# Down projection of a SwiGLU block by seven block products in place of eight, in three chunks between gate/up tiles

## The reference, cut to what matters

```
gate, up = split(rmsnorm(x, g_ffn) @ w_gate_up, 2)      # 1024 -> 2 x 2816
x = x + (silu(gate) * up) @ w_down                      # 2816 -> 1024
```

## Time and profile before

| | us |
|---|---|
| median of 3 runs (1534.44 to 1538.4) | 1536.0 |
| profiled execution, first to last instruction | 1535.0 |
| gate/up and down of layer 0 | about 373 to 779 |
| gate/up and down of layer 1 | about 1100 to 1519 |
| TensorE busy, share of the span | 96% |
| VectorE, ScalarE, GpSimd busy | 43%, 38%, 34% |

### The profile page before, as it was taken

How to read it: one execution, slowest core, us unless ns; L and a number is a source line. 1 busy time by engine, 2 the same in 40 slices (tenths; PEclk the granted TensorE clock), 3 DMA queues, 4 the chain that set the end, 5 groups by cost and what they waited for, 6 DMA issues and landing times.

```text
span 1535.0 us, 27449 instructions
## 1 busy us (share of the span) xinstructions
PE 1471.1 (96%) x10463; PEld 1394.0 (91%) x10463; DVE 656.7 (43%) x1035; ACT 576.1 (38%) x1054; POOL 525.5 (34%) x251
## 2 busy tenths in 40 slices
PE   5899999899999999999999999988999999999996
PEld 5788888699999999999987888868999999999996
DVE  6678777722333333311237666664233333330002
ACT  5454444433222222222235766774422222222211
POOL 1512112134444444344441111112544444443442
PEclk9999999999999999999999999999999999999998
DMA  6223432112222222222231222211222222222231
GB/s 251 72 63 100 130 125 92 56 56 91 81 82 81 81 81 82 86 77 86 78 94 38 89 88 82 71 57 41 83 83 82 82 82 82 82 79 82 83 89 72
DMA packets 42877, 130.25 MB, mean 85 GB/s; under 512 B 5148, under 2 KB 7196, under 8 KB 42688
## 3 DMA queue, kind: packets, MB, share of 16 engines
q1 hardware_dynamic: 38160, 121.23, 26.0%
q10 hardware_dynamic: 4656, 8.21, 1.4%
HBM read 118.85 MB, written 10.57 MB: 84 GB/s over the span
## 4 chain that ended last, share of the span: by engine, by line
PE 83%; DVE 7%; ACT 4%; issue 2%; DMA 1%; DVEq 1%; ACTq 1%; SPq 0%; POOL 0%; POOLq 0%
PE acc L556 72%; PE out_ps L668 4%; PE score L626 3%; PE turned L640 2%; DVE work_c L1160 2%; DMA w_raw<-in_w_in 1%; ACT w_hi L840 1%; PE out_ps L679 1%; DVE work_a L1164 1%; DVE work_a L1157 1%; DVE qz L1133 1%; DVE least L1191 1%; ACT work_c L921 1%; ACT work_c L919 1%; DVE work_b L1198 1%
## 5 line engine op out<-in xcount | busy, mean ns | idle before, releaser
L473 POOL TENSOR_TENSOR w_lo<-w_raw,w_hi 128x1024 fp32r<-128x1024 f32 (+1 forms) x190 | 462.5, 2434 | 856.4 <-ACT w_hi L840 855.9
L556 PE MATMUL acc<-xg_hi,w_hi 128*128 128x288 f32 x2048 | 463.2, 308 | 0.8 <-POOL w_lo L473 0.8
L840 ACT ACTIVATE w_hi<-w_raw 128x1024 fp32r<-128x1024 f32 (+1 forms) x194 | 202.2, 1042 | 640.5 <-PE acc L556 626.4
L556 PE MATMUL acc<-xg_hi,w_lo 128*128 128x288 f32 x2048 | 438.6, 296 | 0.0
L556 PE MATMUL acc<-xg_lo,w_hi 128*128 128x288 f32 x2048 | 437.9, 295 | 0.0
L556 PEld LDWEIGHTS acc<-xg_hi,w_hi 128*128 128x128 f32 x2048 | 332.3, 189 | 20.8 <-issue 13.4
L556 PEld LDWEIGHTS acc<-xg_hi,w_lo 128*128 128x128 f32 x2048 | 329.6, 189 | 0.0
L556 PEld LDWEIGHTS acc<-xg_lo,w_hi 128*128 128x128 f32 x2048 | 329.1, 188 | 0.0
L556 PE MATMUL acc<-f_hi,w_hi 128*128 128x288 f32 x704 | 151.1, 296 | 0.0
L556 PE MATMUL acc<-f_lo,w_hi 128*128 128x288 f32 x704 | 149.8, 293 | 0.0
L556 PE MATMUL acc<-f_hi,w_lo 128*128 128x288 f32 x704 | 148.9, 293 | 0.0
(11 more groups left out here) (148 smaller groups left out, 1620.1 us busy)
## 6 DMA issues: line engine op xcount, KB each, us to landing
w_raw<-in_w_gu SPq DMA_DIRECT2D x88, 512.0 KB, 3.6
w_raw<-in_w_in SPq DMA_DIRECT2D x40, 512.0 KB, 6.0
w_raw<-in_w_dn SPq DMA_DIRECT2D x32, 512.0 KB, 3.5
w_raw<-in_w_out SPq DMA_DIRECT2D x16, 512.0 KB, 3.6
w_raw<-in_w_dn SPq DMA_DIRECT2D x16, 384.0 KB, 3.1
out_k_o<-kb ACTq DMA_DIRECT2D x12, 288.0 KB, 5.1
out_v_o<-vf_z ACTq DMA_DIRECT2D x12, 288.0 KB, 6.9
kb<-in_ck SPq DMA_DIRECT2D x12, 256.0 KB, 2.6
```

The costliest lines, as they stand in the source:

```text
L473: pool.tensor_tensor(w_lo[par][:, 0:cols], raw(s, par, cols), w_hi[par][:, 0:cols].bitcast(F32), ALU.subtract).then_inc(wlo_made, 1)
L556: mm = pe.matmul(acc[:, tpar, h, 0:c1 - c0], w[par][:, k * P:(k + 1) * P], a[:, c0:c1], start=first and n == 0, stop=last and n == 2)
L840: act.activation(w_hi[par][:, 0:cols], raw(s, par, cols), ACT.Copy).then_inc(whi_made, 1)
```

## The change

The input features of the down projection are cut into three chunks of 6, 8 and 8 tiles, and each chunk is multiplied as soon as its gate/up pairs are done: gate/up 0 to 5, down of chunk 0, gate/up 6 to 13, down of chunk 1, gate/up 14 to 21, down of chunk 2. Inside a chunk, each pair of output tiles (4 pairs) is a 2x2 block product: two output tiles by two halves of the chunk's input tiles (3 or 4 tiles each), times two halves of the tokens. Such a product is made of seven block products in place of eight (Strassen, in Winograd's form): the factors are sums and differences of blocks, and the results are added into x piece by piece.

- Weights: three DMAs for each pair bring four blocks of 128 x 384 or 128 x 512 into `d_raw`. GpSimd makes four sums (`d_sum`). For each of the 7 products ScalarE makes `d_hi` and **VectorE** makes `d_lo`, in a ring of three.
- Activations: for an even j VectorE makes one difference of 288 columns, for an odd j a double difference and one more, and ScalarE and VectorE split two blocks (even) or five blocks (odd, 1440 columns) into `f_hi`, `f_lo`. The `high` and `low` of the gate/up slabs stay as they were; the two slabs after a chunk are split around the start of its down products.
- TensorE: a product is 3 x 3 or 3 x 4 matmuls of 288 columns into one bank. Several products accumulate in one bank, and each is added into x by a VectorE operation of 288 columns (`d_add`) before the next goes on top. Loops over gate/up are unrolled on ScalarE and VectorE, and the products are unrolled on all engines.

The diff, cut to its core:

```diff
-DOWN_CUTS = (8, 8, 6)
+CHUNKS = (6, 8, 8)
+CHUNK0 = (0, 6, 14)
...
+PRODUCTS = 7
...
+RING = 3
+QCOLS = 4 * P
...
+    f_hi = sb("f_hi", [P, PRODUCTS, QT, HALF], F32R)
...
+    f_new = sb("f_new", [P, 8, HALF])
+    d_raw = sb("d_raw", [P, 4, QCOLS])
+    d_sum = sb("d_sum", [P, 2, QCOLS])
+    d_hi = sb("d_hi", [P, RING, QCOLS], F32R)
...
+    ADD_TO = ((0, 0), (1, 1), (0, 1), (0, 0), (1, 1), (0, 1), (1, 0))
...
+    def d_bank(pair, r):
+        if r % 2 == 0:
+            return score[:, pair % 2, 0:HALF]
+        return turned[:, 0:HALF] if r == 3 else out_ps[:, 0:HALF]
...
# SyncE, blocks(chunk, m): waits dlo_made and sums_made of the pair before, then
+                sp.dma_start(d_raw[:, 0:2, 0:cols], 
+                             w_dn[layer, 2 * m:2 * m + 2, :, first].rearrange("a p c -> p a c")).then_inc(d_in[0], 16)
...
# GpSimd: first() and second() likewise
+                def third():
+                    pool.wait_ge(dlo_made, pair * PRODUCTS + 2)
+                    pool.wait_ge(sums_made, pair * 4 + 2)
+                    pool.tensor_tensor(one, a11, a21, ALU.subtract).then_inc(sums_made, 1)
...
+                def fourth():
+                    pool.wait_ge(dlo_made, pair * PRODUCTS + 3)
...
+                for t in range(2 * CHUNK0[chunk] + 2, ahead):
+                    if t == ahead - 1:
+                        first()
+                        second()
+                    low(gu_slab(layer) + t, t % 2)
+                third()
+                for t in nxt[0:1]:
+                    low(gu_slab(layer) + t, t % 2)
+                fourth()
+                for t in nxt[1:2]:
+                    low(gu_slab(layer) + t, t % 2)
+                for m in range(1, OUT_PAIRS):
+                    for made in sums(chunk, m):
+                        made()
+                    if chunk == len(CHUNKS) - 1:
+                        for n in range(2 * m - 2, 2 * m):
+                            add_square(2 * layer + 2, n)
...
# TensorE, down(chunk, m), product r
+                    pe.wait_ge(dlo_made, n + 1)
...
+                    elif r == 2:
+                        pe.wait_ge(x_added, pair * PRODUCTS + 1)
+                    elif r == 4:
+                        pe.wait_ge(x_added, pair * PRODUCTS + 3)
...
+                    for k in range(kts):
+                        if m == 0 and r in (0, 2):
+                            pe.wait_ge(flo_made, layer * FT + CHUNK0[chunk] + 2 * k + (1 if r == 0 else 2))
...
# ScalarE
+                own = slice(2, PRODUCTS) if odd else slice(0, 2)
+                src = f_new[:, 3:8, :] if odd else f_new[:, 0:2, :]
+                act.activation(f_hi[:, own, i, :], src, ACT.Copy).then_inc(fhi_made, 1)
...
+            def d_high(chunk, p):
...
+                at_least(act, d_done, n - RING + 1)
...
# VectorE, gate_up(j), after tile_out into work_a and work_c
+                dve.tensor_tensor(prod, halves(work_c[:, 0, :]), halves(work_b[:, 0, :]), ALU.mult)
+                dve.drain()
+                if odd:
+                    own, src = slice(2, PRODUCTS), new(3, 8)
+                    dve.tensor_tensor(new(5, 7), new(4, 5).to_broadcast([P, 2, HALF]), new(1, 3), ALU.subtract)
+                    dve.drain()
+                    dve.tensor_tensor(new(7, 8), new(3, 4), new(5, 6), ALU.subtract).then_inc(prod_made, 1)
...
+                for j in range(CHUNK0[chunk], CHUNK0[chunk] + count):
+                    if j == CHUNK0[chunk] + count - 1:
+                        for p in range(RING):
+                            d_low(chunk, p)
+                    gate_up(j)
+                for p in range(CHUNK_PRODUCTS):
+                    d_add(chunk, p)
+                    if p + RING < CHUNK_PRODUCTS:
+                        d_low(chunk, p + RING)
+                    m, r = divmod(p, PRODUCTS)
+                    if chunk == len(CHUNKS) - 1 and layer < DEPTH - 1 and m and r < 2:
+                        x_low(2 * layer + 2, 2 * m - 2 + r, 1)
```

More of the change, by code:

```diff
@@ L233, in build @@
     flo_made = sem("flo_made")
+    d_in = [sem(f"d_in{i}") for i in range(3)]
+    sums_made = sem("sums_made")
+    dhi_made = sem("dhi_made")
+    dlo_made = sem("dlo_made")
+    d_done = sem("d_done")
+    x_added = sem("x_added")
     x_gained = sem("x_gained")
@@ L439, in _ @@
                             cache(layer, i + 2, par, False)
[L440 to L451, removed]
+            with sp.Fori(0, OUT_TILES // 2) as i:
+                for j in range(2):
+                    slab(i * 2 + (s0 + IN_TILES + j), j,
+                         w_out[layer, bass.ds(i * 2 + j, 1)].rearrange("a p c -> (a p) c"))
@@ new lines, in _ @@
+            for t in range(2):
+                gate_up(t)
+            for chunk, count in enumerate(CHUNKS):
+                ahead = 2 * (CHUNK0[chunk] + count)
+                for t in range(2 * CHUNK0[chunk] + 2, ahead):
+                    gate_up(t)
+                if chunk == 0:
+                    sp.wait_ge(slab_done, gu_slab(layer))
+                    sp.wait_ge(kv_stored, 32 * PAIRS * (layer + 1))
+                blocks(chunk, 0)
+                for t in range(ahead, ahead + 2):
+                    if t < GU_TILES:
+                        gate_up(t)
+                    elif layer < DEPTH - 1:
+                        slab(layer_slab(layer + 1) + t - GU_TILES, t % 2, w_in[layer + 1, t - GU_TILES])
+                for m in range(1, OUT_PAIRS):
+                    blocks(chunk, m)
@@ L539, in _, with sums, first, second @@
-            if layer < DEPTH - 1:
-                add_square(2 * layer + 2, KT - 1)
+            def sums(chunk, m):
+                pair, cols = d_pair(layer, chunk, m), CHUNKS[chunk] * HD
+                a11, a21, a22, a12 = (d_raw[:, n, 0:cols] for n in (0, 1, 2 + pair % 2, 3 - pair % 2))
+                one, two = (d_sum[:, n, 0:cols] for n in range(2))
+                def first():
+                    if pair:
+                        pool.wait_ge(dlo_made, (pair - 1) * PRODUCTS + 5)
+                    pool.wait_ge(d_in[0], 16 * (pair + 1))
+                    pool.wait_ge(d_in[1 + pair % 2], 16 * (pair + 1))
+                    pool.tensor_tensor(one, a21, a22, ALU.add).then_inc(sums_made, 1)
+                def second():
+                    if pair:
+                        pool.wait_ge(dlo_made, (pair - 1) * PRODUCTS + 6)
+                    pool.wait_ge(sums_made, pair * 4 + 1)
+                    pool.tensor_tensor(two, one, a11, ALU.subtract).then_inc(sums_made, 1)
+                def third():
[4 more added lines that the diff above has]
+                    pool.wait_ge(dlo_made, pair * PRODUCTS + 3)
+                    pool.wait_ge(d_in[2 - pair % 2], 16 * (pair + 1))
+                    pool.tensor_tensor(two, a12, two, ALU.subtract).then_inc(sums_made, 1)
+                return first, second, third, fourth
@@ new lines, in _ @@
+            for chunk, count in enumerate(CHUNKS):
+                ahead = 2 * (CHUNK0[chunk] + count)
+                nxt = [t for t in range(ahead, ahead + 2) if t < GU_TILES or layer < DEPTH - 1]
+                first, second, third, fourth = sums(chunk, 0)
+                for t in range(2 * CHUNK0[chunk] + 2, ahead):
+                    if t == ahead - 1:
[8 more added lines that the diff above has]
+                    low(gu_slab(layer) + t, t % 2)
+                for m in range(1, OUT_PAIRS):
+                    for made in sums(chunk, m):
[3 more added lines that the diff above has]
+                            add_square(2 * layer + 2, n)
@@ L541, in _ @@
+            for n in range(KT - 2, KT):
+                if n < KT - 1 or layer < DEPTH - 1:
+                    add_square(2 * layer + 2, n)
         for k in POOL_OUT:
@@ L798, in _ @@
                 product(sg + j, tg + j, j % 2, j % 2, xg_hi, xg_lo)
[L799 to L811, removed]
@@ new lines, in _ @@
+            for chunk, count in enumerate(CHUNKS):
+                first, last = max(1, CHUNK0[chunk] // 2), (CHUNK0[chunk] + count) // 2
+                with pe.Fori(first, last) as i:
+                    for j in range(4):
+                        product(i * 4 + (sg + j), i * 4 + (tg + j), j % 2, j % 2, xg_hi, xg_lo)
+                if chunk == 0:
+                    pe.wait_ge(score_free, attn_use(layer, ATTNS) + 2)
+                    pe.wait_ge(turned_free, 2 * DEPTH + 1 + (layer + 1) * LAYER_ROUNDS)
+                for m in range(OUT_PAIRS):
+                    down(chunk, m)
@@ L1036, in _, with gate_up @@
             sg = gu_slab(layer)
-            def gate_up(j, first=False):
+            def gate_up(j):
                 n = j + (layer * FT + 1)
-                high(j * 2 + (sg + 2), 0)
-                if first:
+                more = j < FT - 1 or layer < DEPTH - 1
+                if more:
+                    high(j * 2 + (sg + 2), 0)
+                if j == 0:
                     factor(attn_use(layer, ATTNS))
@@ new lines, in gate_up, with d_low @@
```

(10 more changed lines are left out.)

175 lines of the change are left out of this document (123 added, 52 removed).

## The result

The changed kernel takes 1553.99 us (median of 4) against 1536.8 beside it: ratio 1.0128 [1.0105, 1.0152], 1.3% slower. It lies in the range (1546 to 1597), 19 us under the 1573 of the prediction. The profiled execution took 1553.6, of which the span (first to last instruction) is 1550.9, 15.9 more than before. The median is 3.1 above that span, where the prediction counted 1.0. One execution of a later kernel, e5, took 2026.1 us at a mean granted clock of 0.66 and is left out of its median and its ratio.

What follows compares the result with a forecast made beforehand. TensorE, 96% busy, was taken as the bound. 1535.0 - 34.8 (removed matmuls) + 36.9 (joints) + 13 (clock) + 22 (inside chunks) = 1572.1, plus 1.0 for the median: 1573 us, range 1546 to 1597.

Steps and rivals of the forecast that it cites:

- Removed work: TensorE in the down stages: 264 matmuls fewer at 0.132 us each, -34.8 us.
- The lock: VectorE operations with two SBUF inputs and GpSimd ones exclude each other for a whole instruction; 2.0 us at a joint.
- The joint: Gate/up to down, six times: TensorE waits before product 2 for `d_add(0)`, 4.3 to 7.0 us each, +36.9 us.
- the chain: At a joint, VectorE's and ScalarE's operations up to `d_add(0)`; TensorE goes on 9.36 us after product 0's start.
- The clock: TensorE's clock falls at the six joint waits and ramps up again, 2.2 us each, +13 us.
- clock holds: Rival: no clock loss behind the joints, 1560 us; chance 0.22, shared with smaller losses inside chunks.
- Inside a chunk: VectorE, held by GpSimd's sums, delays TensorE within chunks: +8, +2, +9 and +3, together +22 us.
- the walk: Product-by-product reckoning; last chunk of layer 0: `d_add(9)` late behind `x_low`, 3.1 us a joint inside the chunk, +9 us.
- At nothing: Inner gate/up pairs' differences and wider `f_hi`, `f_lo`, weight blocks, joint down to gate/up: no cost, as covered.
- Faster: Rival: shorter joint waits (27 us), clock holds, waits inside chunks fall into idle time, 1528 us; chance 0.08.
- It cancels: Rival: joints blocked, 37 us, no clock loss and nothing inside chunks, 1538 us; chance 0.06.
- VectorE bounds every chunk: Rival: each sum holds its `d_low` fully, inside loss 40 us or more, 1591 us with clock loss; chance 0.17.

Runs made afterwards that it cites:

- e5: e1 with VectorE's `x_low` in the last chunk of layer 0 behind products 4 and 5 of a pair, not 0 and 1; 1522.66 us, ratio 0.9908.
- e8: The changed kernel with GpSimd's `w_lo` of the second slab ahead waiting for the last `f_lo`; 1548.58 us, ratio 1.0083.
- e3: The changed kernel with GpSimd's `w_lo` of the second slab ahead waiting for VectorE's last differences; 1549.69 us, ratio 1.0097.
- e2: The changed kernel with `d_add` of a chunk's product 0 moved ahead of VectorE's wait for the last `f_hi`; 1548.19 us, ratio 1.0069.
- e1: The changed kernel with the next chunk's first gate/up slab ahead of the down products, at the ends of chunks 0 and 1; 1523.96 us, ratio 0.9931.
- e4: The changed kernel with 34 unused matmuls between products 1 and 2 at each joint; 1547.22 us, ratio 1.0074.
- e11: e9 with GpSimd's wait for the fifth `d_lo` in the last chunk alone; 1515.46 us, ratio 0.9863.
- e9: e5 plus early `d_add` in the last chunk, GpSimd's `w_lo` behind the fifth `d_lo`, ScalarE's table load behind the sixth `d_hi`; 1518.55 us, ratio 0.9896.

## Why the prediction was right, and where it was off

The direction, the mechanism and the order of the terms were right; the sum for the span was 21 us too high (1572.1 against 1550.9), most of it in one term.

- **Removed work**: 34.8 forecast, 33.3 found, as chunk matmuls start 0.133 us apart, those of before 0.132.
- **The lock**: right in kind, place and size (2.02 us longer in the profile, five joints of six). The Trainium skill ("SBUF — State Buffer", section "Who interferes with whom") says that the second of the two blocks fully. The trace agrees: the locked rows end 0.56 us (`d_lo` in e8), 0.62 (the difference) and 1.51 (`f_lo` in e3) behind the end of GpSimd's operation, each 0.13 to 0.15 us less than it takes by itself. e3 and e8 show that the next operation in line is held in its place.
- **The joint**: 36.9 against 33.4. The steps from one operation to the next were 0.1 to 0.2 us shorter than I had them, 8.83 us for the chain in place of 9.36. The rows of the joint, e2 and e8 show the cause, and e1 shows that other work covers it.
- **The clock**: 13 against 10.8. The six cost 1.4 to 2.7 us each, where I took 2.2; e4 shows the cause. The rival "clock holds" fails.
- **Inside a chunk**: the step that was mis-sized, 22 against 7.5 us, 14.5 of the 21 us of error. I charged VectorE 1.20 us for each product of an 8-tile chunk by adding listed durations. But operations back to back start 0.37 (`d_add`) and 0.60 us (`d_lo`) apart, less than the 0.45 and 0.68 listed: 0.97 against TensorE's 1.60. In the 6-tile chunks it is 0.37 and 0.47, so 0.84 against 1.19, where I had 1.07. GpSimd's sums did hold `d_lo` as forecast: in the first two chunks of layer 0, 11 and 12 of 25 took longer, 4.8 and 6.6 us in all, for 6 and 7.8 forecast. But with that slack the ring of three absorbs them: the 6-tile chunks lost 0.1 us each where I had 4, the second chunks none. This is read from the traces; no run changes VectorE's load there. In the last chunk of layer 0 the walk held (6.6 of 9; `d_add` behind `x_low` was named); e5 shows half of it. In that of layer 1, 0.6 of 3. A slip in the working, without effect on the 9: six squares of 1.47 us are 8.8, where it has 8.5.
- **At nothing**: right for the inner gate/up pairs. The 768 matmuls between two chunks took 102.4 us, 0.133 each, so nothing waits there.
- **The rivals.** "Faster" had its condition right, stalls under 34.8 us; they were 51.7, and e1 and e11, with fewer stalls, are faster than the kernel before. "It cancels" and "VectorE bounds every chunk" fail: the waits at the joints, 33.4 us, use up the 33.3 saved, and the clock and the last chunk of layer 0 make the loss.
- **Not forecast**: the saved work was 1.5 us less, the rest of the span 2.2 shorter and the median 2.1 further above the span. That these nearly cancel is luck.

## What to carry to other kernels

Cutting work on the engine that bounds a kernel can cost more than it saves if the cut adds places where that engine waits for a stage's input (here six, 33.4 us of waits for 33.3 saved). Count the chain from the last product of one stage to the first use in the next, and put an independent piece of the bound engine's work there before adding more stages. When VectorE and GpSimd operations both read two tiles from SBUF, place them against each other; in e3 and e8 a wait added to one only moved the meeting to the next operation in line. Count VectorE's load by start-to-start distances of neighbours, not by listed durations.

## What was not expected of the hardware

- The granted clock fell behind a wait of 1.9 us that followed 4.5 us of full work (e4, first joint of layer 1), and not behind the same wait in layer 0. Behind the same 2.2 us without a matmul in the attention of layer 0 it fell in some executions (before, e4, e5) and not in others (the changed kernel, e1, e9), with the same code there.
- Matmuls that nobody reads made the kernel 6.8 us faster.
- VectorE starts an operation 0.08 us before the listed end of the one before it (0.45 listed, 0.37 apart; 0.68 listed, 0.60 apart).
